# A recurrent and banded-attention encoder layer on one core: the two halves of the recurrence laced into one order, the mixture gates spread over the attention blocks

## The reference, cut to what matters

```python
proj = x @ w_in + b_in
u_lru, g_lru, q, k, v, gate_lru, gate_attn = jnp.split(proj, SPLIT_IDX, axis=-1)
u = depthwise_conv(u_lru, w_lru_conv, b_lru_conv, LRU_CONV_PAD)      # 4 taps, 1280 channels
# for each direction: r, i = sigmoid(block_diag_linear(u, ...)); 8 blocks of 160 channels
#   a = exp(8 r log_sigmoid(lam));  h_t = a_t h_(t-1) + sqrt(1 - a_t^2) i_t u_t
y_lru = ((h_fwd + h_bwd) * gelu(g_lru)) @ w_lru_out
y_attn = windowed_gqa(q, k, v, rel_table, attn_sink) @ w_attn_out    # 8 heads, 2 kv heads, window 128
mix = (sigmoid(gate_lru) * y_lru + sigmoid(gate_attn) * y_attn) @ w_o + b_o
x = layer_norm(ALPHA * x + mix, ln1_g, ln1_b)
# then a gated MLP with a 3-tap depthwise convolution, and a second layer norm
```

## Time and profile before

| | us |
|---|---|
| median of 3 runs | 3126.49 (3125.81 to 3128.97) |
| the profiled execution | 3127.93, its span 3126.0 |
| recurrence of the long sequence, TensorE's first slab to its last | 29.4 to 425.9 |
| attention of the long sequence from TensorE's restart | 429.9 to 831.8 |
| recurrence of the short sequence, from the first slab multiplied ahead | 1997.6 to 2253.9 |
| attention of the short sequence from TensorE's restart | 2269.9 to 2476.0 |

### The profile page before, as it was taken

How to read it: one execution, slowest core, us unless ns; L and a number is a source line. 1 busy time by engine, 2 the same in 40 slices (tenths; PEclk the granted TensorE clock), 3 DMA queues, 4 the chain that set the end, 5 groups by cost and what they waited for, 6 DMA issues and landing times.

```text
span 3126.0 us, 35166 instructions
## 1 busy us (share of the span) xinstructions
PE 2787.5 (89%) x12056; PEld 2278.2 (73%) x12056; DVE 1663.6 (53%) x1749; ACT 784.2 (25%) x1064; POOL 1188.7 (38%) x660
## 2 busy tenths in 40 slices
PE   8968899899799969999999999586799797999996
PEld 5757778778688857888888888465577685777774
DVE  3886754434305145463544635687845343666666
ACT  3655622303200032010110111065522212111110
POOL 2433432121133312333233332464544364566662
PEclk9989999899899979999999999798899898999998
DMA  4232321222754221111111111332323653222221
GB/s 140 80 107 74 109 105 61 88 64 78 280 187 141 74 67 34 50 51 47 40 54 47 54 47 40 122 106 92 117 98 116 228 191 102 68 89 90 90 87 67
DMA packets 115544, 295.43 MB, mean 95 GB/s; under 512 B 11206, under 2 KB 38086, under 8 KB 115464
## 3 DMA queue, kind: packets, MB, share of 16 engines
q1 hardware_dynamic: 51904, 176.84, 17.4%
q10 hardware_dynamic: 63560, 117.56, 10.7%
HBM read 227.77 MB, written 55.57 MB: 91 GB/s over the span
## 4 chain that ended last, share of the span: by engine, by line
PE 74%; DVE 14%; ACT 5%; issue 3%; ACTq 2%; DMA 1%; POOL 1%; DVEq 0%; POOLq 0%
PE ps L580 47%; PE ps L849 13%; PE ps L720 5%; PE ps L635 3%; PE ps L749 2%; PE ps L703 2%; DVE tau L1329 1%; DVE g_conv L1526 1%; DVE small L1475 1%; DVE HH L1536 1%; PE ps L638 1%; DVE sig L1327 1%; DVE ln_out L1564 1%; DVE v_conv L1526 1%; ACTq L1114 1%
## 5 line engine op out<-in xcount | busy, mean ns | idle before, releaser
L505 POOL TENSOR_SCALAR w_head<-raw 128x1024 fp32r<-128x1024 f32 (+2 forms) x304 | 345.0, 1135 | 1836.7 <-PE ps L580 1187.1
L580 PE MATMUL ps<-XH,w_head 128*128 128x512 f32 x2400 | 819.0, 396 | 99.0 <-ACT u_raw L929 54.1
L580 PE MATMUL ps<-XL,w_head 128*128 128x512 f32 x2400 | 813.9, 393 | 0.0
L580 PE MATMUL ps<-XH,w_tail 128*128 128x512 f32 x2400 | 812.6, 393 | 0.0
L506 POOL TENSOR_TENSOR w_tail<-raw,w_head 128x1024 fp32r<-128x1024 f32 (+2 forms) x304 | 772.4, 2541 | 25.4
L580 PEld LDWEIGHTS ps<-XH,w_head 128*128 128x128 f32 x2400 | 457.7, 191 | 204.3 <-issue 58.7
L580 PEld LDWEIGHTS ps<-XL,w_head 128*128 128x128 f32 x2400 | 457.8, 191 | 96.3
L580 PEld LDWEIGHTS ps<-XH,w_tail 128*128 128x128 f32 x2400 | 456.7, 190 | 96.5
L849 PE MATMUL ps<-HH,w_head 128*128 128x512 f32 x576 | 198.9, 399 | 22.5 <-DVE HL L1537 22.5
L1544 DVE TENSOR_TENSOR acc<-ps,acc 128x1024 f32<-128x1024 f32 (+1 forms) x96 | 92.0, 958 | 201.7 <-PE ps L849 197.9
L849 PE MATMUL ps<-HL,w_head 128*128 128x512 f32 x576 | 197.4, 397 | 0.0
(11 more groups left out here) (182 smaller groups left out, 3534.8 us busy)
## 6 DMA issues: line engine op xcount, KB each, us to landing
raw<-w_mlp SPq DMA_DIRECT2D x144, 512.0 KB, 3.3
raw<-w_qkv_mix SPq DMA_DIRECT2D x56, 512.0 KB, 3.4
raw<-w_u SPq DMA_DIRECT2D x20, 512.0 KB, 3.5
raw<-w_g SPq DMA_DIRECT2D x20, 512.0 KB, 3.6
raw<-w_lru SPq DMA_DIRECT2D x16, 640.0 KB, 4.8
gate_dram<-mix_out ACTq DMA_DIRECT2D x16, 512.0 KB, 2.7
gate_in<-gate_dram ACTq DMA_DIRECT2D x16, 512.0 KB, 4.4
raw<-w_attn SPq DMA_DIRECT2D x16, 512.0 KB, 3.2
```

What stands on the lines that cost most here:

```text
L505: order(pool.tensor_scalar(w_head[slot][:, 0:width], raw[raw_slot][:, 0:width], 1.0, 1.0, ALU.mult, ALU.mult))
L580: last = nc.tensor.matmul(bank(group, c), lhs(wl, k), rhs(xl, k, c), start=(k == 0 and n == 0), stop=(k == nk - 1 and n == 2))
```

## The change

`order_of_half` goes. In its place is one list for the whole recurrence and both sequences, `order_lru`, whose entries name kind, half and tile, and all five engines walk it without loops. The second half's tile 0, its rest tile and its tile 1 stand between and behind the last two gate blocks of the first half; the gelu slab of each rest tile stands later, behind g of block 0 and behind g of block 2. `roots` stands ahead of the evacuations of g and u in both sequences. VectorE convolves and splits the second half's rest tile between the first rest tile's decay steps and its recurrence, and ScalarE issues the first stack of the second half behind that. The `tau` buffers alternate by the running number of the tile.

In attention the four slabs ahead of the barrier are now the first kv head's Q slabs, evacuated from PSUM groups 0 to 3; two gate slabs (LEAD) follow V, and the blocks hold 8 of the first kv head and 6 of the second (FILLS). The order of the slab array in DRAM follows.

```diff
-FILL = (16 - EARLY) // KV
+LEAD = 2
+FILLS = (8, 6)
+MIX_AT = (LEAD, LEAD + FILLS[0])
 AHEAD = 2
-KV_SLABS = 6 + FILL
-SLABS = {"lru": 28, "attn": EARLY + KV * KV_SLABS, "y_lru": 8, "y_attn": 8, "w_o": 8, "mlp": NG * 12}
+KV_AT = (0, 6 + LEAD + FILLS[0])
+FILL_AT = (6 + LEAD, KV_AT[1] + 6)
+SLABS = {"lru": 28, "attn": FILL_AT[1] + FILLS[1], "y_lru": 8, "y_attn": 8, "w_o": 8, "mlp": NG * 12}
...
+        def side_user(h, jj, T):
+            back = 2 if is_short(T) else 1
+            k = HALF * h + jj - back
+            return None if k < 0 else 5 * (k // HALF) + k % HALF
+        REST_TILE = HALF
+        order_lru = [("u", 0, REST_TILE), ("u", 0, 0), ("u", 0, 1),
+                     ("gates", 0, 0), ("g", 0, 0), ("u", 0, 2), ("g", 0, REST_TILE),
+                     ("gates", 0, 1), ("g", 0, 1), ("u", 0, 3),
+                     ("gates", 0, 2), ("g", 0, 2), ("u", 1, 0),
+                     ("gates", 0, 3), ("g", 0, 3), ("u", 1, REST_TILE), ("u", 1, 1),
+                     ("gates", 1, 0), ("g", 1, 0), ("u", 1, 2),
+                     ("gates", 1, 1), ("g", 1, 1), ("u", 1, 3),
+                     ("gates", 1, 2), ("g", 1, 2), ("g", 1, REST_TILE),
+                     ("gates", 1, 3), ("g", 1, 3)]
...
-            names = ["u_rest", "u0", "g_rest", "u1"]
-            for j in range(HALF):
-                u_next = [f"u{j + 2}"] if j + 2 < HALF else []
-                names += [f"gates{j}"] + (u_next + [f"g{j}"] if is_short(T) else [f"g{j}"] + u_next)
-            return names
...
-                            if q:
+                            if q and h == 0:
...
+                    for n, (kind, h, jj) in enumerate(order_lru):
+                        if kind == "gates":
+                            load(s0 + n, n % 2, A["w_gate"][HALF * h + jj, :, :], GATEW)
+                            sp.dma_start(gs_raw[:, :], A["w_gate_rest"][HALF * h + jj, :, :]).then_inc(stack_in, 16)
+                            if jj:
+                                moves_of_block(h, jj - 1)
+                        else:
+                            load(s0 + n, n % 2, A["w_" + kind][feature_tile(h, jj), :, :])
...
-                        for n in range(6):
+                        for n in range(EARLY if kv == 0 else 0, 6):
                             g = 6 * kv + n
-                            if g >= 2:
-                                pe.wait_ge(qkv_evac[q], g - 1)
-                            if n < 2:
-                                pe.wait_ge(mix_taken[q], EARLY + FILL * kv if kv else n + 1)
-                                if kv:
-                                    pe.wait_ge(scores_out[q], GROUP * nb * kv)
-                            project(g % 2, T, s0 + EARLY + KV_SLABS * kv + n, g % 2)
+                            pe.wait_ge(qkv_evac[q], g - 1 if kv else n - EARLY + 1)
+                            if kv and n < 2:
+                                pe.wait_ge(mix_taken[q], MIX_AT[kv])
+                                pe.wait_ge(scores_out[q], GROUP * nb * kv)
+                            project(g % 2, T, s0 + KV_AT[kv] + n, g % 2)
+                        if kv == 0:
+                            for m in range(LEAD):
+                                pe.wait_ge(qkv_evac[q], 2 + m + 1)
+                                project(2 + m, T, s0 + 6 + m, m % 2)
                         pe.wait_ge(qkv_evac[q], 6 * kv + 6)
                         if kv:
                             pe.wait_ge(pt_split[q], pt_before(nb, nb))
                         else:
-                            pe.wait_ge(mix_taken[q], EARLY)
+                            pe.wait_ge(mix_taken[q], LEAD)
...
-                            if n * per_block >= FILL:
+                            if n * per_block >= FILLS[kv]:
...
+                        if jj == REST_TILE:
+                            if h:
+                                act.wait_ge(input_gated[q], 5)
...
-                            decays(4 * h + jj, jj, [side(r, jj, T) for r in sig[0:2]])
-                            def take_u():
-                                if jj < HALF - 2:
-                                    take_channels(jj + 4, 4 * h + jj + 2, u[jj % 2], [(raw_read[q], 5 * h + jj + 3)])
-                            def take_g():
-                                take_projection(side(gelu_g, jj, T), ACT.Gelu_apprx_tanh, col("b_g", 4 * h + jj),
-                                                [(y_ready[q], tiles_before + 1 - lag(jj, T))])
-                            if is_short(T):
-                                take_u()
-                                take_g()
+                            decays(h, jj, [side(r, jj, T) for r in sig[0:2]])
                             if jj == HALF - 1:
-                                store_y(act, q, T, 4 * h + jj - 1, tiles_before - 1, jj - 1)
-                            roots(jj)
-                            if not is_short(T):
-                                take_g()
-                                take_u()
-                        tiles_before = 5 * h + 4
+                                store_y(act, q, T, h, jj - 1)
+                            if h and jj == 0:
+                                store_y(act, q, T, 0, REST_TILE)
+                            roots(h, jj)
+                            if jj < HALF - 1:
+                                for e in behind_gates(h, jj):
+                                    take(*e)
+                        take("g", h, HALF - 1)
                         act.wait_ge(rest_moved[q], 64 * (HALF * h + HALF + 1))
-                        decays(8 + h, HALF, [r[:, 0:T] for r in sigr[0:2]])
-                        store_y(act, q, T, 4 * h + 3, 5 * h + 3, 3)
-                        roots(HALF)
-                        store_y(act, q, T, 8 + h, 5 * h + 4, HALF)
+                        decays(h, REST_TILE, [r[:, 0:T] for r in sigr[0:2]])
+                        if h == 0:
+                            take("u", 1, REST_TILE)
+                        roots(h, REST_TILE)
+                        store_y(act, q, T, h, HALF - 1)
+                        if h == 0:
+                            take("u", 1, 1)
+                            stack_rests(act, q, T, 1, 0)
+                    store_y(act, q, T, 1, REST_TILE)
...
+                    convolve(0, REST_TILE)
+                    split_channels(0, REST_TILE)
+                    convolve(0, 0)
+                    split_channels(0, 0)
+                    convolve(0, 1)
+                    for h in range(2):
                         for jj in range(HALF):
-                            tile_no = 5 * h + jj
                             blk = HALF * h + jj
-                            if jj < HALF - 1:
-                                dve.wait_ge(slab_done, s0 + 14 * h + slab_in_half(T, f"gates{jj}") + 3)
-                                split_channels(jj + 3, u[(jj + 1) % 2], u_head, u_tail)
+                            if blk < BLOCKS - 1:
+                                dve.wait_ge(slab_done, s0 + slab_at[("gates", h, jj)] + 3)
+                                split_channels((blk + 1) // HALF, (blk + 1) % HALF)
                             dve.wait_ge(gate_evac[q], 5 * blk + 4 + 2)
                             r_i = [side(z, jj, T) for z in sig]
-                            decay_steps(tile_no, jj, r_i[0:2], r_i[2:4], u[jj % 2])
-                            if jj < HALF - 2 and is_short(T):
-                                convolve(f"u{jj + 2}", jj + 4, u[jj % 2])
-                            recur(tile_no, jj, r_i[0:2], r_i[2:4], side(gelu_g, jj, T), f"g{jj}")
-                            if jj < HALF - 2 and not is_short(T):
-                                convolve(f"u{jj + 2}", jj + 4, u[jj % 2])
+                            decay_steps(h, jj, r_i[0:2], r_i[2:4], u[jj % 2])
+                            recur(h, jj, r_i[0:2], r_i[2:4], side(gelu_g, jj, T))
+                            if jj < HALF - 1 and blk + 2 < BLOCKS:
+                                convolve((blk + 2) // HALF, (blk + 2) % HALF)
                         dve.wait_ge(rest_moved[q], 64 * (HALF * h + HALF + 1))
                         r_i = [z[:, 0:T] for z in sigr]
-                        decay_steps(5 * h + 4, HALF, r_i[0:2], r_i[2:4], ur)
-                        recur(5 * h + 4, HALF, r_i[0:2], r_i[2:4], gelu_gr[:, 0:T], "g_rest")
+                        decay_steps(h, REST_TILE, r_i[0:2], r_i[2:4], ur)
+                        if h == 0:
+                            convolve(1, REST_TILE)
+                            split_channels(1, REST_TILE)
+                        recur(h, REST_TILE, r_i[0:2], r_i[2:4], gelu_gr[:, 0:T])
+                        if h == 0:
+                            convolve(1, 1)
...
+                        if kv == 0:
+                            for m in range(LEAD):
+                                mix_gate(m, s0 + 6 + m, psum(2 + m, T))
+                            for m in range(LEAD):
+                                store_mix_gate(m)
```

349 lines of the change are left out of this document (159 added, 190 removed).

## The result

The changed kernel takes 3052.71 us (3051.77 to 3053.15, 4 runs) against 3127.07 (3125.81 to 3128.97): the ratio is 0.976, 95% interval 0.974 to 0.978. That is 74.4 us less; 3054 was forecast. The forecast of the time was right to 1.3 us, and two terms of its sum were wrong by 18 and 19 us in opposite directions. Most of what follows is about those two.

What follows compares the result with a forecast made beforehand. Time could only come out of TensorE's waits and the slow clock behind them. Gains 26.6 + 23.8 + 16.6 + 5.6 = 72.6 us off 3127.9 give 3055.3, less 1.4 for the median: 3054, range 3036 to 3076.

Steps and rivals of the forecast that it cites:

- Part 1: Long recurrence: reordering slabs so the second half starts inside the first half's tail gains 26.6 us.
- M3: Start of the fifth evacuation of the first half's last gate block: forecast 185.6 long, 2104.4 short.
- M0: Start of the fifth evacuation of the first half's first gate block: forecast 77.7 long, 2041.5 short.
- M4: Start of the fifth evacuation of the second half's first gate block: forecast 246.0 long, 2144.5 short.
- M7: Start of the fifth evacuation of the second half's last gate block: forecast 344.6 long, 2204.5 short.
- Part 2: Short recurrence: the new order, with roots straight behind the decays, gives two-slab periods of 20 us; gain 23.8 us.
- rival (d): VectorE becomes the bound: one more operation per block takes its long form, 27 us, total 3081; chance 0.11.
- Part 3: Attention's first key-value head: fillers in every block remove waits and slow clock; 16.6 us long, 5.6 us short.
- Part 4: Loops over the recurrence's halves written as straight code: at most 3 us gain, as much loss allowed, taken as nothing.
- (b): Deeper gain: short-sequence periods fall to 18 us and DMA landings are short, total 3038; chance 0.14.
- (c): No lacing: gates (1,0) wait in effect for the rest tile's whole recurrence, a ScalarE step being late; 3072; chance 0.09.
- (e): Slower: VectorE's recurrence drifts into GpSimd's splits in every block; 3176 with four long operations a block; chance 0.04.

Runs made afterwards that it cites:

- the loops alone: The kernel before with its five engines' loops over the recurrence's halves written out as straight code, nothing else changed: 3109.13 us against 3126.93.
- experiment 3: Two variants of the changed kernel (3052.71 us), short sequence: old order inside a period, 3054.70 us; GpSimd's subtraction of the weights' tail left out, 3023.84 us.

## Why the prediction was right, and where not

**Part 1, the long lacing: right, mechanism and size.** Forecast M3 near 186, a wait of 16 before gates (1,0) on `u_stack`, periods of 42.2 and twice 32.85. Measured M3 182.13, the wait 15.57, periods 42.2, 32.6, 32.6. The boundary was forecast at 38.2 + 4.2 + 2.5 + 1.9 + 2 = 48.8 from M3; it was 48.2. VectorE, ScalarE and TensorE there:

```profile
220.55 3.93 DVE L1295 SCALAR_TENSOR_TENSOR ur<-u_raw,cols,ur 128x1024 f32<-128x1024 f32 x3
224.51 1.11 ACT L914 ACTIVATE u_raw<-ps,cols 128x1024 f32<-128x1024 f32 x1 [2.91 <-DVE ur L1295]
...
227.71 0.61 ACTq L428 DMA_DIRECT2D u_stack<-ur_head  x1
230.35 1.19 PE L629 MATMUL ps<-u_head,w_head 128*128 128x512 f32 x2 [15.57 <-DMA u_stack<-ur_head]
```

The convolution starts M3 + 38.4, takes 3.93, ScalarE's part ends with the third issue at 228.32, and the landing takes 2.0. Less the 7.3 us of the loops the long recurrence gained 25.5 for 26.6. TensorE's restart, forecast near 403, came at 397.1. Of the 6.2 us beyond the forecast 3.0 stand at M0 already, and with the loops alone M0 comes as much earlier, at 85.57 instead of 88.55 (0.8 of it a quicker first load, which differs between executions). Another 1.9 stand between M4 and M7, forecast as 98.55 and measured as 96.65; the loops alone take 1.1 off there, and the last of these periods is 31.4 and not a full one.

**Part 2, the short lacing: the mis-sized term.** Forecast 23.8; measured 14.0, of which 9.4 are the loops, so the lacing gave 4.6. The step that failed is "I take 20 for them, since VectorE's work for a block in contention with GpSimd is nearly as long". The periods without the first one's third slab were 19.9, 27.3, 17.8, 27.9 and 17.5, 22.1 in the mean, near the ceiling of 22.5. It set the periods by work taken as fixed, and that work grew: VectorE's from 205 to 223 us over the stretch, 10 of the 18 us already with the loops alone. Without the subtraction the same periods are 17.9 in the mean, so the subtraction is worth 4 us a period. Over the six periods the forecast was 10.4 us too short, which is the whole of the 9.8 between 14.0 and 23.8. This is rival (d), in the short sequence only: VectorE became the bound. A second thing is missing from the step: it counts waits, and on top of the straight code the lacing removed none here. TensorE's idle time went from 74.8 to 75.9 us, its busy time from 188.1 to 182.4, so what the lacing did give came as clock. That the roots' new place gains 2.4 us a period was wrong in the total (experiment 3). The boundary was right: 33.1 us from M3 to gates (1,0), as forecast, with a wait of 14.1 where 15 to 18 were expected.

**Part 3, the mixture gates: right.** 16.6 and 16.6, 5.7 for 5.6; run alone it gave 24.5, and the long second head has some 2 us of the rest: its first 4 us ran at a clock of 0.58 before and run at 1.00 after.

**Part 4, writing out: the other mis-sized term.** Forecast 0, with 3 either way; measured 17.8. The failing step is the row it was read from: gaps of "0.1 us an operation or less" between VectorE's operations from 240.66 to 245.59 (their mean is 0.1, and two of the four are above 0.14). VectorE's loop costs nothing clear of noise, and ScalarE, which hands PSUM groups back to TensorE, was not looked at. The register instructions stand in the trace of before, 16 of them at L982 and 64 at L978.

**The rivals.** (b), a deeper gain, did not come; its periods of 18 us do come without GpSimd's subtraction, which is worth 28.9 us. (c) did not happen. (e), VectorE drifting into GpSimd's splits, is the mechanism seen in the short sequence, at a seventh of its price (17.7 us of VectorE's work for 122).

That the total came out right is luck: 19 us too much for the short lacing and 18 too little for the loops met. A forecast of 3054 for the lacing and the fillers alone, without the loops, would have missed by 16 us (72.6 against 74.4 - 17.8 = 56.6).

## What to carry to other kernels

Here an operand addressed by a loop's register cost a register instruction behind the wait, about 0.1 us on an operation that TensorE waits for, and 13.5 us in all. Where an engine evacuates PSUM on the critical path, look in the trace for register instructions at those lines before giving a loop no price. Where VectorE and GpSimd run side by side, VectorE's busy time is no constant: it was 205 to 223 us for the same work in different orders, so bound a period with the longer forms. Where the clock moves, count TensorE's busy time beside its idle time: four kernels here took waits away from the short recurrence of after, and its stretch got longer, because the same matmuls took longer. Split a large edit into its parts and run each alone even when the sum came out as forecast.

## What the runs showed of the hardware

The register instruction takes 46 ns, runs behind the wait and not during it, and with it the sigmoid starts 0.10 us later (0.14 against 0.04 us behind TensorE's last matmul). A scan of 128 x 1024 that takes 2.29 us on VectorE took 4.32 beside GpSimd's split, and the same 194 or 195 VectorE instructions took 205, 211, 215 or 223 us in different orders, 177 without GpSimd's subtractions. TensorE's same instructions in the short recurrence took 182.4 us at a mean granted clock of 0.88 with the waits gathered in two periods, and 194.4 at 0.85 with them spread, although it stood 10 us less; two other profiles with the gathered order have 183.7 and 184.3. The three moves of `u_stack` landed 2.0 us behind the end of the last issue, in the sequence of 1024 columns.
